# Two chained transformer models on one core: the first model's input projections in one block with split operands, norms and rotations woven in, the head norm by diagonals, paired latent heads

## What is computed

```python
def first_block(x, c, ctx, c_ctx, ...):
    for l in range(DEPTH):                       # 2
        mod = (jax.nn.silu(c) @ w_ada[l] + b_ada[l]).reshape(b, 1, N_MOD, D_MODEL)
        u = modulate(rms_norm(h, g_norm1[l]), mod[:, :, 0], mod[:, :, 1])     # and uc for the context
        pl = jnp.split(u @ w_in[l], IN_SPLITS, axis=-1)                        # widths 512 512 512 | 256 128 32 | 512 128 128
        ya, ya_c = diff_attention(pl[0:3], pc[0:3], ...)   # 4 heads: softmax(q1 k1) - lam * softmax(q2 k2), rms_norm over each head's 128
        yb, yb_c = mla(pl[3:6], pc[3:6], ...)              # latents -> rms_norm -> 8 heads, score = nope (64) + rope (32)
        yw, yw_c = window_gqa(pl[6:9], pc[6:9], ...)       # 8 query heads on 2 key heads, band of 128
        h = h + mod[:, :, 2] * merge_branches(u, (ya, yb, yw), ...)
        ...                                                # conv_ffn; the same for the context in layer 0
```

## Time and profile before

| | before |
|---|---|
| median of 2 runs | 4436.16 us (4433.94 to 4438.38) |
| profiled execution | 4430.6 us, span 4428.8 us |
| granted TensorE clock, mean | 0.951 |
| PE busy | 3967.1 us, 90% |
| DVE / ACT / POOL busy | 51% / 36% / 7% |

### The profile page before, as it was taken

The page is one execution under the profiler, slowest core; times in us unless marked ns, Lnnn a source line. Parts: engine busy times, 40 slices in busy tenths (PEclk is TensorE's granted clock), DMA queues, the critical chain, the costliest instruction groups (busy, mean ns, idle before and its releaser), DMA issues. The chain is left out here.

```text
span 4428.8 us, 52386 instructions
## 1 busy us (share of the span) xinstructions
PE 3967.1 (90%) x19294; PEld 2992.2 (68%) x19294; DVE 2280.5 (51%) x3774; ACT 1574.0 (36%) x2663; POOL 320.8 (7%) x292
## 2 busy tenths in 40 slices
PE   4996988999899888986989989979979998988998
PEld 2653656777788787653666678857658886657886
DVE  7877575223554374075362355435655535564552
ACT  2044525112343254034351234324344423353431
POOL 1201010000000000000000010011210000401001
PEclk8997999999999999998999999989989999989999
DMA  6602030111222244100002223322112332202332
GB/s 234 218 8 71 1 118 22 57 57 59 72 99 98 88 160 140 51 14 24 21 22 85 90 81 95 103 71 75 58 48 86 95 101 86 81 15 81 95 103 78
DMA packets 83411, 349.69 MB, mean 79 GB/s; under 512 B 9152, under 2 KB 9280, under 8 KB 79680
## 3 DMA queue, kind: packets, MB, share of 16 engines
q1 hardware_dynamic: 69440, 297.48, 20.6%
q0 software_dynamic: 13824, 50.34, 3.4%
HBM read 345.68 MB, written 2.10 MB: 79 GB/s over the span
## 5 line engine op out<-in xcount | busy, mean ns | idle before, releaser
L565 DVE TENSOR_TENSOR split_low<-weight_ring,split_high 128x1024 fp32r<-128x1024 f32 (+1 forms) x412 | 547.1, 1328 | 752.2 <-ACT split_high L557 751.9
L557 ACT ACTIVATE split_high<-weight_ring 128x1024 fp32r<-128x1024 f32 (+1 forms) x430 | 479.6, 1117 | 948.9 <-PE banks L1097 466.8
L1225 PE MATMUL banks<-normed_high,split_high 128*128 128x512 f32 (+1 forms) x1760 | 653.7, 371 | 78.9 <-DVE normed_low L449 37.9
L1225 PE MATMUL banks<-normed_low,split_high 128*128 128x512 f32 (+1 forms) x1760 | 651.1, 370 | 0.0
L1225 PE MATMUL banks<-normed_high,split_low 128*128 128x512 f32 (+1 forms) x1760 | 650.7, 370 | 0.0
L1225 PEld LDWEIGHTS banks<-normed_high,split_high 128*128 128x128 f32 x1760 | 334.5, 190 | 140.1 <-issue 84.2
L1225 PEld LDWEIGHTS banks<-normed_low,split_high 128*128 128x128 f32 x1760 | 334.8, 190 | 55.7
L1225 PEld LDWEIGHTS banks<-normed_high,split_low 128*128 128x128 f32 x1760 | 334.4, 190 | 55.2
L1097 PE MATMUL banks<-hidden_high,split_high 128*128 128x512 f32 (+1 forms) x880 | 325.0, 369 | 7.3 <-DVE split_low L565 7.3
L1097 PE MATMUL banks<-hidden_high,split_low 128*128 128x512 f32 (+1 forms) x880 | 324.4, 369 | 0.0
L1097 PE MATMUL banks<-hidden_low,split_high 128*128 128x512 f32 (+1 forms) x880 | 324.4, 369 | 0.0
(11 more groups left out here) (237 smaller groups left out, 6408.6 us busy)
## 6 DMA issues: line engine op xcount, KB each, us to landing
weight_ring<-in_up SPq DMA_DIRECT2D x220, 512.0 KB, 3.5
weight_ring<-in_down SPq DMA_DIRECT2D x80, 704.0 KB, 4.0
modulation_ring<-in_ada POOLq DMA_DIRECT2D x96, 512.0 KB, 4.5
weight_ring<-in_merge SPq DMA_DIRECT2D x48, 768.0 KB, 4.3
weight_ring<-in_out SPq DMA_DIRECT2D x32, 512.0 KB, 3.5
weight_ring<-in_diff SPq DMA_DIRECT2D x12, 1024.0 KB, 5.2
weight_ring<-in_xbc SPq DMA_DIRECT2D x16, 512.0 KB, 3.5
weight_ring<-in_window SPq DMA_DIRECT2D x6, 1024.0 KB, 4.9
```

The lines of the kernel that those rows point to most:

```text
L557: act.activation(k.splits[0][:, (n0 + panel) % RING, 0:width], k.slot(n0 + panel)[:, 0:width], ACT.Copy).then_inc(k.high_ready.sem, 1)
L565: dve.tensor_tensor(k.splits[1][:, s, 0:width], k.ring[:, s, 0:width], k.splits[0][:, s, 0:width].bitcast(F32), ALU.subtract).then_inc(k.l ...
L1225: last = pe.matmul(sums(r, half), w, x, start=(c + j == 0), stop=(c == KT - 1 and j == 2))
```

## The change

`mix_branches` no longer calls `stream_norm`, `project`, `rope`, `norm` and `copy_tiles`, and three window panels, six differential and two latent ones become 22 panels of 512 KB: four for the differential values, eighteen of 128 outputs each. One block, `project_inputs`, takes them all. It holds the stream norm (split in chunks of 128 features, each normed, shifted, rounded to high and low as the products want it), 144 value matmuls, 18 tile jobs of 24 split matmuls per region, the sums of squares and the norms of the latents, and the rotation of 14 tiles.

```diff
+            for c in range(KT):
+                panel = c // 2
+                pe.wait_ge(*k.low_ready(panel + 1))
+                pe.wait_ge(*k.normed_ready(2 * (c + 1)))
+                weights = split_parts(k, n0, panel, c % 2 * 512, 512)
+                for t in range(6):
+                    units = highs[:, c, t * P:(t + 1) * P], lows[:, c, t * P:(t + 1) * P]
+                    for j, (u, w) in enumerate(triple(units, weights)):
+                        last = pe.matmul(k.psum[:, 2 + t, :], u, w, start=(c + j == 0), stop=(c == KT - 1 and j == 2))
...
+            for q in range(TILE_JOBS):
+                panel = VALUE_PANELS + q
+                pe.wait_ge(*k.low_ready(panel + 1))
+                if q == 1:
...
+                for s, (a, b) in enumerate(regions(q)):
+                    for c in range(KT):
+                        for j, (w, u) in enumerate(triple(split_parts(k, n0, panel, c * P),
+                                                          (highs[:, c, a:b], lows[:, c, a:b]))):
+                            last = pe.matmul(bank(q, s), w, u, start=(c + j == 0), stop=(c == KT - 1 and j == 2))
+                    if s == len(regions(q)) - 1:
+                        last.then_inc(k.product_ready.sem, 1)
+                    if s == 0:
+                        if q == 2:
+                            sum_latents(2, queried, 0)
+                        if q == 4:
+                            pe.wait_ge(*k.deviation_ready(2 + len(queried)))
+                            sum_latents(1, columns, 2)
...
+            def rotate(q):
+                i, rows = q - ROPE_KEY, targets[q][:, CTX:T]
+                dve.wait_ge(*k.rope_swapped(i + 1))
+                if i >= 1:
+                    dve.wait_ge(*k.roped(i))
+                dve.tensor_tensor(k.probs[:, 1, 0:LAT], swap_bank(q), k.table(f"sin_{table(q)}"),
+                                  ALU.mult).then_inc(k.sine_part.sem, 1)
+                dve.wait_ge(*k.cosine_part(i + 1))
+                dve.wait_ge(*k.sine_part(i + 1))
+                dve.tensor_tensor(rows, k.probs[:, 0, 0:LAT], k.probs[:, 1, 0:LAT], ALU.add).then_inc(k.roped.sem, 1)
```

```diff
+            def finish_head(h):
+                pe.wait_ge(*k.diagonal_ready(h + 1))
+                if h >= 1:
+                    pe.wait_ge(*k.head_stored(len(queried) * h))
+                for block_ in range(lo, 6):
+                    at = block_ * P
+                    out = k.psum[:, 7, at:at + P] if block_ < 2 else k.psum[:, 6, at - CTX:at - CTX + P]
+                    last = pe.matmul(out, mixed[:, h, at:at + P], k.probs[:, h, at:at + P], start=True, stop=True)
+                last.then_inc(k.head_turned.sem, 1)
...
                     for j in range(per):
-                        last = pe.matmul(result(t)[rows * j:rows * j + rows, :], step["values"][j][c],
-                                         turned[(per * t + j) % slots][0:size, c * P:(c + 1) * P],
-                                         start=(step["first"] and c == 0),
+                        weights = turned[(per * t + j) % slots][0:size, c * P:(c + 1) * P]
+                        operands = (weights, step["values"][0][c]) if combined else (step["values"][j][c], weights)
+                        out = result(t) if combined else result(t)[64 * j:64 * j + 64, :]
+                        last = pe.matmul(out, *operands, start=(step["first"] and c == 0),
...
+            def square(t):
+                act.wait_ge(*k.output_stored(t + 1))
+                if t >= 12:
+                    act.wait_ge(*k.squares_ready(t - 11))
+                act.activation(scratch[:, t % 12, :], steps[t]["out"], ACT.Square,
+                               accum_out=steps[t]["square"]).then_inc(k.squares_ready.sem, 1)
...
+        for at, end in q_tiles:
+            maps = []
+            for j, rows in enumerate(halves):
+                turn = slice(64 * j + 32 * (pair % 2), 64 * j + 32 * (pair % 2) + 32)
+                maps.append(segments(mixed[rows, 4 + pair, at:at + P], keys[rows, pair, :], 0, end, ends=False)
+                            + segments(rope_queries[turn, pair // 2, at:at + P], latents[turn, 3, :], 0, end,
+                                       begins=False))
```

```diff
+    @block.scalar
+    def _(act):
+        if ada:
+            act.wait_ge(*k.prep_loaded(16))
+            act.activation(k.cond, k.cond, ACT.Silu).then_inc(k.prep_scalar.sem, 1)
+        split_ahead(k, act, 1)
...
+        if ada:
+            sp.dma_start(k.cond, k.inp["cond"]).then_inc(k.prep_loaded.sem, 16)
...
+                tiles += 1
+
         def body(i, final):
             step = 0
...
                     split_low(k, dve, n0, q + 1, gate_width, k.high_ready(i * 6 + (q + 2)))
+                if ada:
+                    modulate_until(ada * (6 * i + q + 1) // count)
                 target = merged[:, bass.ds(i * 2 + q // 3, 1), :].rearrange("p a b -> p (a b)")
...
-            def split(block, source):
-                split_tiles(k, block, *([t[:, c, a:b] for c in range(KT)] for t in (source, highs, lows)))
...
-                split(block, normed)
-
-                merge(k, block, l, mixed, highs, lows, normed, context)
+                merge(k, block, l, mixed, highs, lows, merged, context, ada)
```

768 lines of the change are left out of this document (470 added, 298 removed).

## The result

The changed kernel takes 4335.92 us (median of 2 runs, 4333.03 to 4338.81). The ratio to before is 0.9769 with a 95% interval of 0.9753 to 0.9785: 2.3% faster. The forecast was 4330 us in a range from 4295 to 4378. Measured once more beside the experiments, the same kernel took 4330.27 us (5 runs), ratio 0.9763, interval 0.9750 to 0.9776.

The account below looks back on a forecast made before the run. PE was taken as the bound, busy 90% of the span, full in projections but waiting in norms, rotations and copies. Layer 0 -52 and layer 1 -55 make -107 of 4430.6: 4324, plus 5.5 gives 4330; range 4295 to 4378.

Parts of the forecast that it names:

- Prices of matmuls: In project_inputs: split matmuls 0.229 us (512 columns), 0.120 (256); tile jobs 8.4 or 5.5 us, permutations 0.95 each.
- Splits, stores, rotations at nothing: In the tile jobs: ACT, DVE and POOL work hides behind the job's matmuls and adds 0 us.
- Start and norm: Layer 0: modulation begins 2.5 us later, first product at 73.1 instead of 74.93; layer 1: chunked norm saves 5.2 us.
- Latents in one block: Latent norms, up-projection, rotation and copies: 36 us instead of 85.1 in layer 0 (-49), 29.5 instead of 67.6 in layer 1 (-38).
- Differential attention: Steps without woven products take 5.12 us, squares lie in slack: -9 us in layer 0, -14 in layer 1.
- Rival 2: Differential steps do not shorten, as woven products filled waits or squares delay exponentials: +23 us, time 4353; chance 0.09.
- MLA attention: Large step 6.4 us instead of 5.50, with a second score pair of 32 rows: +16 us layer 0, +14.4 layer 1.
- Rival 1: MLA's 32-row score pair does not run side by side, 1.3 us more per large step: +45, time 4375; chance 0.10.
- Merge: Layer 0 merge start waits for 1 MB and Silu, plus 0.8 for biases: +7.4 us; layer 1 start -0.8.
- The 128 products: Layer 0 merge: modulation products on DVE, about 1.3 us each, 166 us, hidden by the gate products.
- Rival 4, the lower clock: PE in project_inputs falls to the lower clock: slower than before, wholly there 4708 us; chance 0.05.

Follow-up runs that it names:

- plain-matmul experiment: Changed kernel with one plain f32 matmul of the high parts in place of each split triple in project_inputs: 4410.20 us, ratio 0.9937.
- the filler: Changed kernel with one useless plain f32 matmul of 384 columns behind every differential attention step, results in one bank: 4318.56 us, ratio 0.9730.
- the second execution: Second profiled execution of the unedited changed kernel: span 4325.5 us, against 4330.8 in the first.
- the early split: Changed kernel with ScalarE's first split of weights in the merge put ahead of Silu and its wait: 4323.28 us, ratio 0.9758.

## Why the prediction was right, point by point

- *Prices of matmuls.* Right. Jobs are 9.19 us apart where 8.4 + 0.95 was said, and the short ones of layer 1 6.34 where 5.54 + 0.95 was said: 0.15 too much on each. The plain-matmul experiment gave 83 us for the 80 of the same prices. Over two layers the projections were reckoned 8 us too dear, of which these 36 jobs are 5.
- *Splits, stores, rotations at nothing.* Right. No gap stands between jobs, and put behind them the rotations cost 31 us.
- *Start and norm.* Right within 1 us in both layers, in layer 0 partly by luck: modulation began 4.0 us later (its first product at 19.96 instead of 15.95) where a middle of 2.5 had been chosen, and then waited less for its transfers, so that it ended 2.3 later.
- *Latents in one block.* 37.6 and 28.0 us for 36 and 29.5.
- *Differential attention.* The step that failed, in layer 0: "Without products behind the steps a step is 5.12 us", and from it -9. Measured +1.8, and about +0.3 in the other execution. The chain was reckoned right, as the filler shows: at a clock of 0.97 to 1.0 the stage has 114.4 to 117.3 us of matmuls, where 114.6 was said for the stage. What was not reckoned is that the products taken out were also what held the clock: 0.98 with them, 0.87 and 0.90 without, 0.97 with filler in their place. In layer 1 the clock rose after some steps and stayed (1.00 from 1910 on): 91.9 for 89.8. The row behind the 5.12 was from layer 1, where steps are all large and PE waits 1.42 us in each. In layer 0 PE waits 2.07 and 2.31 us where a cycle passes from its small steps to large ones, and in the second execution the scores behind the longer of these waits took 2.77 us instead of 1.56 (at 317.04). That these waits are what lets the clock fall was not tested apart. Rival 2 thus happened in half, by another mechanism than its two: the products had not filled waits, and the squares cost nothing.
- *MLA attention.* The loop was right, the size a little off: 6.61 us a large step for 6.4, as the second pair stands with 1.49 us and not 1.3. That is 3.4 us in each layer. The rest of the 7.6 us by which layer 1 missed is its start at half the clock; in the second execution, where the clock came back sooner, the stage took 113.8 us instead of 118.5, for 111 forecast. Rival 1 is out: the pair of 32 rows ran side by side.
- *Merge.* The start was +6.6 in the forecast, 5.8 measured (10.9 for 5.1 behind the attention); the early split gives that back. The 128 products are hidden, as said. The stage that ends in the merge's start came out lower still (+3.7 and -3.9 for +6.6 and -0.8), and the difference is what the window attentions are shorter (2.1 and 3.4 us, at a clock of 1.00 for 0.96 and 0.92), a term that the forecast did not have.
- *Rival 4, the lower clock.* In the projecting blocks 0.99. The clock did cost time, but in the differential attention of layer 0 (124.3 and 122.8 us from first to last matmul, 114.4 to 117.3 with filler), and the forecast had looked for it in the projections only.

In the profiled execution the projections were reckoned 8 us too dear, the differential and MLA attentions 23 us too cheap (10.8 and 2.1, 2.9 and 7.6), and the window attentions with the merge's starts 6 us too dear. That leaves the 9 us between -107 and -98. The mechanisms of the projections, the merge and the MLA loop held; that the total came out so near is in part luck, as misses of 37 us in all cancelled down to 9.

## What to carry to other kernels

Where work is taken out from behind a chain of engines, read the granted clock of the stretch and not only the wait: what was taken out may be what held the clock, and here a cheap matmul that computes nothing gave the loss back. A stage that waits for one reciprocal or one rotation at a time is best woven into a stage that is full of matmuls; there it costs its own matmul and nothing else. At a stage's start, look at what stands ahead of the one instruction that everybody waits for: a load and an activation whose first reader, a product on DVE, came at 687.02, 3.9 us behind PE's first matmul, held PE back by 6.6 us.

## What the runs showed of the hardware that was not expected

- TensorE can be busy without a break and still be granted the lower clock: 0.69 and 0.81 on average over 165 us of busy PE. In the first of these windows 120 of the 165 us were score matmuls on 64 and 32 rows, one head at a time. With the same scores two heads side by side, the MLA window of layer 0 has 0.98. Which property of the work makes the difference was not tested.
- Once fallen behind a wait of 3 us, the clock stayed at 0.50 for 15 us, in which PE was busy for 13.8, mostly with such score matmuls.
- Between two executions of the same kernel, the clock fell at the same place for 15 us in one and was back within 6 in the other: 186.5 against 181.9 us for the same two attentions, most of the 5 us between the spans.
- Two heads of 64 rows side by side take exactly the time of one (1.49 us for eight records and for four), and so do two of 32 rows.
